# One decoder step with three-term products: tokens split at 320, and the last 256 columns of the high and low part taken by one instruction

## The reference, cut to what matters

```python
a = rmsnorm(h, norm_mix_g)                       # 576 x 1024
z = a @ w_in                                     # q, k, v of two branches, gates mo, gg, ga, gb
hm = head_layernorm(mlstm_scan(...)) * g_mnorm * sigmoid(mo)
hg = head_rmsnorm(gla_scan(...)) * g_gnorm * silu(gg)
merged = sigmoid(ga) * (hm @ w_pa) + sigmoid(gb) * (hg @ w_pb)
h = h + merged @ w_o
c = rmsnorm(h, norm_ffn_g)
u_gate, u_val = split(c @ w_up)                  # 2 x 2688 columns
h = h + (silu(conv3(u_gate) + conv_b) * u_val) @ w_down
e = rmsnorm(h, norm_ple_g)
h = h + sigmoid(e @ w_ple_gate) * (p @ w_ple_proj)
y = rmsnorm(h, final_norm_g)
```

## Time and profile before

| | |
|---|---|
| median of 3 runs | 1249.86 us (1247.95 to 1251.46) |
| the profiled execution | 1247.99 us, span 1246.1 us |
| PE busy | 1206.3 us, 97% of the span, 9115 matmuls |
| VectorE busy | 751.2 us, 60% |
| ScalarE busy | 383.5 us, 31% |
| mean DMA rate | 111 GB/s |

### The profile page before, as it was taken

How to read it: one execution, slowest core, us unless ns; L and a number is a source line. 1 busy time by engine, 2 the same in 40 slices (tenths; PEclk the granted TensorE clock), 3 DMA queues, 4 the chain that set the end, 5 groups by cost and what they waited for, 6 DMA issues and landing times.

```text
span 1246.1 us, 21519 instructions
## 1 busy us (share of the span) xinstructions
PE 1206.3 (97%) x9115; PEld 1171.1 (94%) x9115; DVE 751.2 (60%) x1409; ACT 383.5 (31%) x512; POOL 2.3 (0%) x7
## 2 busy tenths in 40 slices
PE   7999999989999999999999999999999999999996
PEld 6999989879999998988999999999999999999995
DVE  7722467546888876655555566666666663233666
ACT  5322122243343333123343323322223222111533
POOL 0000000000000000000000000000000000000000
PEclk9999899999999999999999999999999999999998
DMA  6133102423223136754443443122222224222212
GB/s 227 69 123 115 37 32 85 148 97 130 68 101 97 63 114 216 237 178 154 157 155 107 147 166 112 68 97 73 74 97 69 91 68 168 89 88 91 102 68 77
DMA packets 48319, 138.74 MB, mean 111 GB/s; under 512 B 5068, under 2 KB 24524, under 8 KB 39008
## 3 DMA queue, kind: packets, MB, share of 16 engines
q1 hardware_dynamic: 15896, 89.77, 21.4%
q10 hardware_dynamic: 32328, 47.60, 11.1%
HBM read 113.55 MB, written 23.81 MB: 110 GB/s over the span
## 4 chain that ended last, share of the span: by engine, by line
PE 86%; DVE 6%; issue 4%; ACT 2%; DMA 2%; ACTq 0%; POOL 0%; DVEq 0%; POOLq 0%; SPq 0%
PE ps L686 58%; PE ps L692 9%; PE ps L755 3%; PE ps L756 3%; PE ps L760 2%; PE aux L932 2%; PE ps L713 1%; DVE wlo L993 1%; DMA out_C_s<-st 1%; PE aux L884 1%; ACT whi L1642 1%; PE aux L948 1%; PE aux L857 1%; PE aux L894 1%; PE aux L942 0%
## 5 line engine op out<-in xcount | busy, mean ns | idle before, releaser
L686 PE MATMUL ps<-ahi,whi 128*128 128x288 f32 x1584 | 343.8, 299 | 10.8 <-ACT ahi L1734 8.2
L686 PE MATMUL ps<-alo,whi 128*128 128x288 f32 x1584 | 340.6, 297 | 0.0
L686 PEld LDWEIGHTS ps<-ahi,whi 128*128 128x128 f32 x1584 | 256.4, 190 | 14.6 <-issue 11.8
L686 PEld LDWEIGHTS ps<-alo,whi 128*128 128x128 f32 x1584 | 255.0, 189 | 0.0
L993 DVE TENSOR_TENSOR wlo<-wraw,whi 128x2048 fp32r<-128x2048 f32 (+2 forms) x89 | 191.0, 2146 | 91.1 <-ACT whi L1642 86.9
L1642 ACT ACTIVATE whi<-wraw 128x2048 fp32r<-128x2048 f32 (+2 forms) x89 | 159.3, 1789 | 148.0 <-PE ps L686 122.1
L686 PE MATMUL ps<-ahi,wlo 128*128 128x288 f32 x832 | 179.1, 297 | 0.0
L686 PEld LDWEIGHTS ps<-ahi,wlo 128*128 128x128 f32 x832 | 134.9, 190 | 0.0
L692 PE MATMUL ps<-ahi,wlo 128*128 128x288 f32 x752 | 107.8, 296 | 0.9 <-DVE wlo L993 0.9
L692 PEld LDWEIGHTS ps<-ahi,wlo 128*128 128x128 f32 x752 | 102.8, 189 | 1.1 <-DVE wlo L993 1.1
L755 PE MATMUL ps<-whi,ahi 128*128 128x256 f32 (+1 forms) x320 | 80.3, 288 | 0.0
(11 more groups left out here) (348 smaller groups left out, 1643.1 us busy)
## 6 DMA issues: line engine op xcount, KB each, us to landing
wraw<-in_w_in SPq DMA_DIRECT2D x32, 1024.0 KB, 5.2
wraw<-in_w_up SPq DMA_DIRECT2D x21, 1024.0 KB, 4.9
gate_scratch<-stg ACTq DMA_DIRECT2D x32, 288.0 KB, 4.6
gt<-gate_scratch ACTq DMA_DIRECT2D x32, 288.0 KB, 3.3
wraw<-in_w_pgate SPq DMA_DIRECT2D x6, 1024.0 KB, 4.8
wraw<-in_w_down SPq DMA_DIRECT2D x8, 704.0 KB, 4.0
wraw<-in_w_down SPq DMA_DIRECT2D x8, 640.0 KB, 3.9
out_C_s<-st ACTq DMA_DIRECT2D x16, 256.0 KB, 3.4
```

The source lines that it names most:

```text
L686: mm = nc.tensor.matmul(ps[:, t % 2, a, 0:HALF], w, x(k)[:, a * HALF:(a + 1) * HALF], start=f, stop=e)
```

## The change

`product` is replaced by `wide_product` for the kinds in `WIDE`: `ga`, `gb`, `pa`, `pb`, `wo`, both tiles of `up`, and `down`. The tokens are split at CUT = 320 and not at 288. Part a (tokens 0 to 319) is three matmuls of 320 columns into one bank. For part c (tokens 320 to 575) the high and the low activations are read by one matmul of 2 x 256 columns with the weight whi, into the 512 columns of the other bank; hi·wlo of part c (256 columns) is added to the first 256 of them. A block is so five matmuls (320, 320, 512, 320, 256) with 1728 columns in all, as many as six of 288. The tile is not yet the product: the two halves of the second bank are still to be added. VectorE does it at the release: by a sum over pairs into `csum` for most kinds, by one more addition for `wo` and `down`. High and low parts get a common tensor (`ahl`, `hmlh`, `mghl`, `achl`), at the addresses they had.

```diff
+CUT = 320
+WIDE = ("ga", "gb", "pa", "pb", "wo", "gate", "val", "up", "down")
...
+            def wide_product(t, blocks, hi, pair, s, start=True, stop=True, ready=None, mid={}, low_part=None):
+                a, c = ps[:, t % 2, 0, 512 - CUT:], ps[:, t % 2, 1, 0:T - CUT]
+                both_c = ps[:, t % 2, 1, 0:2 * (T - CUT)].rearrange("p (e x) -> p e x", e=2)
+                for n, (col, k) in enumerate(blocks):
...
+                    nc.tensor.matmul(a, wh, x[:, 0:CUT], start=first, stop=False)
+                    nc.tensor.matmul(a, wh, x_lo[:, 0:CUT], start=False, stop=False)
+                    nc.tensor.matmul(both_c, wh, x_both, start=first, stop=False)
+                    if not low_part:
+                        nc.tensor.matmul(a, wl, x[:, 0:CUT], start=False, stop=last)
+                        mm = nc.tensor.matmul(c, wl, x[:, CUT:], start=False, stop=last)
...
             def evac(kind, i, t):
                 dve.wait_ge(tile_ready, t + 1)
                 full, fr = tile(t), tile_free[t % 2]
+                if kind in WIDE:
+                    full = flat(t)
+                    part_a, part_c = full[:, 0:CUT], ps[:, t % 2, 1, :]
+                    if kind not in ("wo", "down"):
+                        link(V.reduce_sum(csum[:, :], part_c.rearrange("p (e x) -> p x e", e=2), axis=mybir.AxisListType.X))
...
+                        V.tensor_tensor(stg[:, k % 2, CUT:], csum[:, :], rs[:, CUT:], ALU.mult)
+                        V.tensor_tensor(stg[:, k % 2, 0:CUT], part_a, rs[:, 0:CUT], ALU.mult).then_inc(fr, 1)
...
                 elif kind == "pa":
                     g = gt_take()
-                    V.tensor_tensor(two(merged[:, i, :]), full, two(gt[:, g % NGT, :]), ALU.mult).then_inc(fr, 1)
+                    V.tensor_tensor(merged[:, i, CUT:], csum[:, :], gt[:, g % NGT, CUT:], ALU.mult)
+                    V.tensor_tensor(merged[:, i, 0:CUT], part_a, gt[:, g % NGT, 0:CUT], ALU.mult).then_inc(fr, 1)
...
-                    V.tensor_tensor(two(x), full, two(xr[:, i % 2, :]), ALU.add).then_inc(fr, 1)
+                    link(V.tensor_tensor(x, full, xr[:, i % 2, :], ALU.add))
+                    V.tensor_tensor(x[:, CUT:], x[:, CUT:], part_c[:, T - CUT:], ALU.add).then_inc(fr, 1)
...
-                    V.tensor_tensor(gbuf[:, 2:2 + HALF], p0[:, 0:HALF], rsv[:, 0:HALF], ALU.mult)
-                    V.tensor_tensor(gbuf[:, 2 + HALF:2 + TP], p1[:, 0:n1], rsv[:, HALF:TP], ALU.mult)
+                    V.tensor_tensor(gbuf[:, 2 + CUT:2 + TP], csum[:, 0:TP - CUT], rsv[:, CUT:TP], ALU.mult)
...
+                    V.tensor_tensor(gbuf[:, 2:2 + CUT], part_a, rsv[:, 0:CUT], ALU.mult).then_inc(fr, 1)
```

More of the change, by code:

```diff
@@ L505, in tile, with flat @@
             return ps[:, t % 2, :, 0:HALF]
+        def flat(t):
+            return ps[:, t % 2, :, :].rearrange("p a b -> p (a b)")[:, 512 - CUT:512 - CUT + T]
         def bcast(ap, n, where_):
@@ L738, in _ @@
                         slot(t)
-                        product(t, [(b * P, b) for b in range(11)], rows_of(achi), rows_of(aclo), u % 2, stop=False,
-                                ready=((ff_hi, 0), (ff_lo, 0)) if i == 0 else None).then_inc(half_done, 1)
+                        wide_product(t, [(b * P, b) for b in range(11)], rows_of(achi), ac_pair, u % 2, stop=False,
+                                     ready=((ff_hi, 0), (ff_lo, 0)) if i == 0 else None).then_inc(half_done, 1)
                 elif s[0] == "tile":
@@ L763, in _ @@
                     elif kind == "down":
-                        product(t, [(b * P, 11 + b) for b in range(10)], rows_of(achi), rows_of(aclo), w, start=False,
-                                ready=((ff_hi, 0), (ff_lo, 0)) if i == 1 else None)
+                        wide_product(t, [(b * P, 11 + b) for b in range(10)], rows_of(achi), ac_pair, w, start=False,
+                                     ready=((ff_hi, 0), (ff_lo, 0)) if i == 1 else None)
                     elif kind == "pproj":
@@ L786, in _ @@
                             pe.wait_ge(split_lo, u + 1)
-                        product(t, [(k * 2 * P + n * P, k) for k in range(KT)], hi, lo, w, ready=ready, mid=mid,
-                                low_part=u + 1 if n == 0 and not ready else None)
+                        (wide_product if kind in WIDE else product)(
+                            t, [(k * 2 * P + n * P, k) for k in range(KT)], hi, lo, w, ready=ready, mid=mid,
+                            low_part=u + 1 if n == 0 and not ready else None)
                 elif s[0] == "bt":
@@ L1128, in evac @@
                 elif kind == "val":
-                    V.tensor_tensor(two(vrs[:, :]), full, two(rsv[:, :]), ALU.mult).then_inc(fr, 1)
+                    V.tensor_tensor(vrs[:, CUT:], csum[:, :], rsv[:, CUT:], ALU.mult)
+                    V.tensor_tensor(vrs[:, 0:CUT], part_a, rsv[:, 0:CUT], ALU.mult).then_inc(fr, 1)
                     dve.wait_ge(ff_sg, i + 1)
@@ L1146, in evac @@
                     x = h2[:, i, :]
-                    V.tensor_tensor(two(x), full, two(x), ALU.add).then_inc(fr, 1)
+                    link(V.tensor_tensor(x, full, x, ALU.add))
+                    V.tensor_tensor(x[:, CUT:], x[:, CUT:], part_c[:, T - CUT:], ALU.add).then_inc(fr, 1)
                     dve.wait_ge(fr, t // 2 + 1)
```

68 lines of the change are left out of this document (49 added, 19 removed).

## The result

The changed kernel takes **1253.69 us** in the median of 20 runs (1249.55 to 1257.2), the kernel before 1249.34 us in 20 runs beside them (1246.59 to 1253.22). The ratio is 1.0035, interval 1.0026 to 1.0043: slower by 4.4 us, where 2.1 us less were forecast. The time lies inside the range, the direction is wrong.

What follows compares the result with a forecast made beforehand. PE was taken to bound the kernel, busy 97% of the span, with other engines' chains pacing `ga` to `pa`. 4.26 + 1.56 - 8.4 + 0.46 = -2.1 us gave a median of 1247.7 us, range 1239 to 1255.

Steps and rivals of the forecast that it cites:

- the saving per block: Every PE block: one matmul less saves its fixed 13.3 ns, 800 to 786.7 ns, with 226.7 ns for 512 columns.
- step 6: `pb` to `down`, where PE alone sets the pace: 58 tiles and `down` save 8.4 us.
- Steps 1 to 3: `ga` and `gb` tiles from 467 to 575.94 us: PE's delay changes by +0.4, +0.25 and -0.53 us.
- Step 4: Chain of VectorE and ScalarE from 575.94 to 648.11 us, through `pa`: longer releases add 4.14 us before `pb` starts.
- The releases hide: Rival: the chain in `pa` has unseen slack, the wait ahead of `pb` is about 2.5 us; 1243.5 us, chance 0.15.
- Step 5: Behind PE's 5.1 us wait ahead of `pb`: the clock falls to 1.2 GHz for 3.4 us, +1.56 us.
- The sum is not dear: Rival denied here: the pair sum takes 1.22 us, VectorE bounds `up`; 1262.8 us, chance 0.12.
- The long matmul is not cheap: Rival denied here: 512 columns cost 216.7 ns, 10 ns less in each block that counts; 1240.6 us, chance 0.15.
- The rival that decides "from 229.7 ns on": The matmul reading two far pieces pays for both; at 240 ns PE saves nothing, 1257.2 us; chance 0.10.

Runs made afterwards that it cites:

- e1: Changed kernel with the 512 columns read in one piece of the high part, so the result is not the product: 1254.15 us, ratio 1.0037 to before.
- e5: Changed kernel with a second, equal pair sum in every second `pa` tile, those whose release starts behind `wlo` without a wait: 1257.67 us, ratio 1.0075.
- e6: Changed kernel with a second, equal pair sum in the other `pa` tiles, where VectorE mostly waits for its gate: 1254.84 us, ratio 1.0039.
- e7: Changed kernel with 18 products of ones, 128 columns each, ahead of the first `pb` block, while PE waits: 1252.6 us, ratio 1.0033.
- e4: Change only in `ga`, `gb` and `pa`; `pb`, `wo`, `up`, `down` as in the kernel before: 1256.89 us, ratio 1.0059.
- late alone: Change only in `pb`, `wo`, `up` and `down`; `ga`, `gb`, `pa` as in the kernel before: 1246.28 us, ratio 0.9966.
- e12: Change only in `pb`, `wo`, `up`, `down`, 7 products of ones ahead of the wait at 538, a block's last two matmuls exchanged: 1244.65 us, ratio 0.9966.

## Why the prediction was wrong

- **The step that failed is the saving per block**, "512/2.4 + 13.3 = 226.7 ns, which I take", and with it 13.3 ns a block. The mechanism was right, the size was off: the 512 columns cost 230.9 and the block's first matmul 149.1, so a block saves 6.7 ns (16.80 us to 16.66 for a `down` tile of 21 blocks; 12.80 to 12.69 for a full unit of `up`). `pb` to `down` gives back 3.5 us where step 6 had 8.4. That is 4.9 of the 6.5 us between forecast and result; 4.2 of them are the smaller saving of 632 blocks. Another 0.3 is a wait that was put at nothing: at the border of `pb` and `wo` PE's next start comes 0.40 us behind the last one (708.79 to 709.19), where 256 columns take 0.12; before, there is no such gap (699.37). The last 0.4 was not traced. The line through 256, 288 and 320 columns was taken 192 columns further than its last point, and all three points came from runs in which PE did nothing but equal lengths; the five matmuls of unlike length beside each other were bounded on the 512 alone.
- **Steps 1 to 3** were too kind: +0.9, +0.8 and -0.2 in place of +0.4, +0.25 and -0.53 (the third from e1, C to the release at 579.18: 37.48 against 37.71 us). Part of it is the same 13.3 ns, credited to the ten `ga` and `gb` tiles of steps 2 and 3 (1.06 us; half of that at the measured saving). In the first step the measured delay lies at or above the 0.78 that was the upper bound, not at the middle; what the remaining 0.1 to 0.3 us in each of the first two is was not tested.
- **Step 4 held**: 575.94 to 648.11 became 579.78 to 656.35, +4.40 us for +4.14, and e5 and e6 show that it is the releases behind `wlo` that count, one in a pair. The releases hide: falls.
- **Step 5 held** in its effect: 0.50 behind the wait, 506.4 to 506.9 us from D to E against 504.9, so 1.5 to 2.0 us for 1.56; e7 shows that the standing still is the cause. That the clock falls only behind the wait did not hold: it fell inside it.
- **The sum is not dear** (688 ns), VectorE keeps 0.59 us in `up`. **The long matmul is not cheap**: it costs 230.9 ns. The Trainium skill ("TensorE: Matmul & The Clock Gate", "Back-to-back issue gap") gives N/2.4 + 2.5 ns, 215.8 ns for it, as the gap of an isolated matmul; the trace doesn't agree for this stream.
- Sum with the measured terms: +6.0 up to D (forecast 4.26), +1.7 for the clock (1.56), -3.5 (-8.4), +0.2 behind E (0.46): **+4.4 us**, against 4.4 between the medians. That it comes out to the tenth is luck: each term is from a few single profiles, known to 0.2 to 0.3 us, and the falls behind C, which come and go by 1.5 us, are not in it. The forecast for A to D alone, 5.8 with its clock, lies inside the interval of e4 (+5.2 to +9.6 us).
- The chances: the direction turned on a difference of two terms of 6 and 8 us. The rival that decides "from 229.7 ns on" had 0.10, and a middle case, half the saving, had no place of its own. That the time lies inside the range is owed to the range's width: the forecast's own went from 1245 to 1250.

## What to carry to other kernels

Fewer instructions on the engine that bounds a stage pay there and nowhere else; where a chain over the other engines sets the pace, the same edit pays only its extra release. Apply such a change by stage: late alone it is 0.34% faster, everywhere it is 0.35% slower. With the stall at 538 filled by idle products as well, one version was 0.5% faster (1243.35 us in 5 runs) and its sister e12 0.3% (9 runs).

A fixed cost per instruction that is read from runs of equal lengths is not the saving when lengths are mixed: bound the whole new sequence, neighbours and all, and not only the new instruction.

Before a loss or gain of 1.5 us is given to a change, look at a second trace of the kernel before: the granted clock behind waits of 1.7 to 1.9 us falls in one trace and not in the next.

## What the runs showed of the hardware that was not expected

- A float32r matmul of 512 columns costs 231 ns start to start, from one piece (230.7) or from two pieces far apart (230.9) alike; with it in a block, 3.3 to 6.7 ns above the line are paid in all, less when the 256-column one stands directly behind it (790.0 against 793.3 ns).
- Four matmuls of 384 and one of 192 columns cost 807 ns, six of 288 cost 800: the one behind 192 columns takes 188 ns in place of 173.3. A 320 behind a 256 costs 149 to 151, and where the two alternate the 256 give it back with 117.
- The granted clock can fall inside a wait of 4.9 us (0.67 in 652:656 with PE idle), and a fall costs nothing where another engine's chain sets the pace (64.8 us from the first `pa` block to D with and without).
- Idle products keep the granted clock at 1.00 over a wait of 4.9 us, but what was the clock's loss partly turns into the next wait (1.0 of 1.6 us came back).
